# One product per block in a convolution over frequencies, and column halves for the last rows of three output projections

## What is computed

```python
def rms_norm_2(x, g):
    xf = x.astype(jnp.float32)
    y = xf * lax.rsqrt(jnp.mean(xf * xf, axis=-1, keepdims=True) + RMS_EPS)
    return (y * g.astype(jnp.float32)).astype(x.dtype)
...
    u = a_val * jax.nn.sigmoid(a_gate)
    u = depthwise_conv_centred(u, conv_w, conv_b)
...
    y = jnp.concatenate([y_a, y_b], axis=-1) @ w_out
    return x + rms_norm_2(y, g_post)
```

## Time and profile before

| | |
|---|---|
| median of 3 runs | 897.77 us |
| the profiled execution's own time | 897.9 us |
| its span, first to last instruction | 896.1 us |
| PE busy | 865.1 us, 97% of the span |
| DVE busy | 533.7 us, 60% |
| ACT busy | 487.8 us, 54% |
| mean granted clock of PE | 0.992 of full speed |

### The profile page before, as it was taken

How to read it: one execution, slowest core, us unless ns; L and a number is a source line. 1 busy time by engine, 2 the same in 40 slices (tenths; PEclk the granted TensorE clock), 3 DMA queues, 4 the chain that set the end, 5 groups by cost and what they waited for, 6 DMA issues and landing times.

```text
span 896.1 us, 15443 instructions
## 1 busy us (share of the span) xinstructions
PE 865.1 (97%) x6204; PEld 787.0 (88%) x6204; DVE 533.7 (60%) x947; ACT 487.8 (54%) x819; POOL 18.5 (2%) x23
## 2 busy tenths in 40 slices
PE   8999999999999999999899999999999799999996
PEld 7999898879689999988699998899988699998785
DVE  5344347757666666666765344268775654548664
ACT  6653456763474445454653244746675565445453
POOL 0000000006100000000000000000000000000000
PEclk9999999999999999999999999999999999999999
DMA  9655732335445555555445244333436454535211
GB/s 363 254 183 191 282 139 95 112 125 198 150 138 184 188 189 188 185 187 193 141 147 183 94 142 142 129 132 122 157 120 244 140 176 154 189 101 181 95 48 70
DMA packets 21698, 144.53 MB, mean 161 GB/s; under 512 B 2529, under 2 KB 3169, under 8 KB 4992
## 3 DMA queue, kind: packets, MB, share of 16 engines
q1 hardware_dynamic: 20736, 140.55, 45.3%
q10 hardware_dynamic: 896, 3.03, 1.0%
HBM read 142.53 MB, written 1.05 MB: 160 GB/s over the span
## 4 chain that ended last, share of the span: by engine, by line
PE 87%; DVE 5%; ACT 4%; DMA 2%; issue 1%; DVEq 0%; ACTq 0%
PE PS L424 85%; DVE wl L1672 2%; ACT wh L1153 2%; DMA ring<-w 1%; ACT PB L1187 1%; DMA xa<-x 0%; PE PS L1069 0%; ACT hh L1167 0%; PE PS L695 0%; DVE PB L2155 0%; PE PS L697 0%; PE PS L696 0%; DVE PB L1715 0%; DVE hl L1692 0%; DVE cn L1976 0%
## 5 line engine op out<-in xcount | busy, mean ns | idle before, releaser
L1672 DVE TENSOR_TENSOR wl<-ring,wh 128x1024 fp32r<-128x1024 f32 x248 | 305.6, 1235 | 293.5 <-ACT wh L1153 293.2
L1153 ACT ACTIVATE wh<-ring 128x1024 fp32r<-128x1024 f32 x248 | 261.5, 1056 | 269.1 <-PE PS L424 250.6
L424 PE MATMUL PS<-hh,wh 128*128 128x256 f32 x1244 | 359.1, 289 | 2.5 <-DVE hl L1729 2.2
L424 PE MATMUL PS<-hl,wh 128*128 128x256 f32 x1244 | 352.5, 283 | 0.0
L424 PE MATMUL PS<-hh,wl 128*128 128x256 f32 x1244 | 352.4, 283 | 0.0
L424 PEld LDWEIGHTS PS<-hh,wh 128*128 128x128 f32 x1244 | 238.9, 192 | 8.1 <-issue 5.4
L424 PEld LDWEIGHTS PS<-hl,wh 128*128 128x128 f32 x1244 | 239.0, 192 | 1.4 <-issue 1.2
L424 PEld LDWEIGHTS PS<-hh,wl 128*128 128x128 f32 x1244 | 238.9, 192 | 0.0
L424 PE MATMUL PS<-wh,hh 128*128 128x256 f32 (+2 forms) x496 | 171.0, 345 | 5.2 <-DVE hl L1692 4.1
L424 PE MATMUL PS<-wl,hh 128*128 128x256 f32 (+2 forms) x496 | 166.9, 337 | 0.0
L424 PE MATMUL PS<-wh,hl 128*128 128x256 f32 (+2 forms) x496 | 166.9, 337 | 0.0
(11 more groups left out here) (266 smaller groups left out, 710.2 us busy)
## 6 DMA issues: line engine op xcount, KB each, us to landing
ring<-w SPq DMA_DIRECT2D x127, 1024.0 KB, 4.8
cn<-consts SPq DMA_DIRECT2D x2, 1051.0 KB, 9.5
V<-gains ACTq DMA_DIRECT2D x3, 512.0 KB, 6.2
cn<-consts SPq DMA_DIRECT2D x1, 1050.5 KB, 9.1
xa<-x SPq DMA_DIRECT2D x2, 512.0 KB, 4.5
ring<-w SPq DMA_DIRECT2D x2, 512.0 KB, 5.8
out<-xb SPq DMA_DIRECT2D x4, 256.0 KB, 2.1
cn<-late ACTq DMA_DIRECT2D x1, 704.0 KB, 8.1
```

Of the source, the lines that this page charges most:

```text
L424: return nc.tensor.matmul(o, lhsT, rhs, start=start, stop=stop, skip_group_check=True)
L1153: A(wh[:, q % SPLITS, :], ring[:, i % RING, e:e + HALF], ACT.Copy).then_inc(sem("hi_ready"), 1)
L1672: TTn(wl[:, q % SPLITS, :], ring[:, PLACE[unit_of(q)] % RING, e:e + HALF], wh[:, q % SPLITS, :].bitcast(F32), ALU.subtract).then_inc(sem(" ...
```

## The change

In the convolution DVE makes the sum that PE made: it multiplies the spectrum by `WF[0]` into `z`, multiplies each half of the partitions by `WF[1]` into the other half of `turned`, and adds `turned` to `z`. The sign moves into the table `conv_tap`. `conv_inverse` has one matmul where it had two. The second set is done at i == 1 of the loop, ahead of the gate biases, instead of at i == 2 behind them.

In the three output projections the last rows of t = 1 are done by column halves: h = 0 for the last three halves of weights (`first_rows` again), then h = 1 with the releases. ACT squares each column half by itself (`part_square`); DVE adds epsilon to the first half's sum (`part_bias`), and the root takes that as its bias (`part_root`). At two joins the split of the next matrix's first half goes behind the norm's work on ACT (`down`) and on DVE (`down` and `even_out`).

```diff
             def deep(first, a, b, bank):
...
+            def deep_last_rows(first, rest, bank):
+
+                for k in rest:
+                    m = deep_part(first, k, 1, 0, bank)
+                m.then_inc(sem("first_rows"), 1)
+                for k in rest:
+                    half_out(deep_part(first, k, 1, 1, bank))
...
-                        for k in range(2):
-                            m = mm(PS[:, AV[i % 2], e * S + o:e * S + o + n], PRODUCT[i // 2][:, b, k, q:q + P],
-                                   c("conv_inv", k * BLOCK, k * BLOCK + n), k == 0, k == 1)
+                        m = mm(PS[:, AV[i % 2], e * S + o:e * S + o + n], PRODUCT[i // 2][:, b, 0, q:q + P],
+                               c("conv_inv", 0, n), True, True)
...
+            def part_square(m, h, src):
+
+                o = (spare if m == 3 else xh[:, 1, :])[:, h * 512:(h + 1) * 512]
+                A(o, src, ACT.Square, scale=D ** -0.5,
+                  accum_out=ssq[:, TT * m + 1:TT * m + 2] if h else stat[:, 42 + m % 2:43 + m % 2])\
+                    .then_inc(sem("row_ssq[1]"), 1)
+
+            def part_root(m):
+
+                act.wait_ge(sem("row_ssq[1]"), PARTS_DONE[m, 1])
+                act.wait_ge(sem("row_bias"), m)
+                A(rms[:, TT * m + 1:TT * m + 2], ssq[:, TT * m + 1:TT * m + 2], ACT.Sqrt,
+                  bias=stat[:, 44 + m % 2:45 + m % 2]).then_inc(sem("row_rms[1]"), 1)
...
-            act.wait_ge(sem("first_rows"), 3)
+            act.wait_ge(sem("first_rows"), 4)
             row_square(4, 0, PS[:, EVEN_AT:EVEN_AT + 2, :])
             row_root(4, 0)
+            act.wait_ge(sem("first_rows"), 5)
+            part_square(4, 0, PS[:, EVEN_AT + 2, :])
             halves(half_of("lora") + 1)
             act.wait_ge(sem("half_used"), half_of("even_out") + 16)
-            row_square(4, 1, PS[:, EVEN_AT + 2:EVEN_AT + 4, :])
-            row_root(4, 1)
-            for t in range(TT):
-                act.wait_ge(sem("x4_ready"), t + 1)
-                row_square(5, t, cols2(xa[:, t, :]))
-                row_root(5, t)
+            part_square(4, 1, PS[:, EVEN_AT + 3, :])
+            part_root(4)
+            act.wait_ge(sem("x4_ready"), 1)
+            row_square(5, 0, cols2(xa[:, 0, :]))
+            row_root(5, 0)
+            for h in range(2):
+                act.wait_ge(sem("x4_ready"), h + 2)
+                part_square(5, h, xa[:, 1, h * 512:(h + 1) * 512])
+            part_root(5)
...
-                    for i in range(2):
-                        ins = TTn(PRODUCT[h][:, b, i, :], PS[:, 3 + b, :], WF[i][h], ALU.mult)
-                    ins.then_inc(sem("conv_weighed"), 1)
+                    z, turned = PRODUCT[h][:, b, 0, :], PRODUCT[h][:, b, 1, :]
+                    own(TTn(z, PS[:, 3 + b, :], WF[0][h], ALU.mult))
+                    for lo in (0, SPAN):
+                        q, o = slice(lo, lo + SPAN), slice(SPAN - lo, P - lo)
+                        own(TTn(turned[o], PS[q, 3 + b, :], WF[1][h][q], ALU.mult))
+                    settled()
+                    TTn(z, z, turned, ALU.add).then_inc(sem("conv_weighed"), 1)
...
                 halves(half_of("qk") + i + 1 + SPLITS)
+                if i == 1:
+                    weigh_spectrum(1)
                 if i == 2:
...
-                if i == 2:
-                    weigh_spectrum(1)
...
-            for t in range(TT):
-                gained(6, DEEP, t)
-                post_norm(6, t, xa, xb, "out_ready", 2)
+            gained(6, DEEP, 0)
+            post_norm(6, 0, xa, xb, "out_ready", 2)
+            part_gained(6, DEEP, 0)
+            part_bias(6)
+            part_gained(6, DEEP, 1)
+            post_norm(6, 1, xa, xb, "out_ready", 2)
...
-    put_conv("conv_tap", np.concatenate([cos, cos, sin, sin], 1))
+    put_conv("conv_tap", np.concatenate([cos, cos, sin, -sin], 1))
     cos, sin = (q.T / P for q in turn(np.arange(BLOCK)))
-    put_conv("conv_inv", np.concatenate([np.concatenate([cos, -sin]), np.concatenate([-sin, -cos])], 1))
+    put_conv("conv_inv", np.concatenate([cos, -sin]))
```

More of the change, by code:

```diff
@@ L299, in program @@
         xh = PBF[:, 0:TT * D].rearrange("p (t d) -> p t d", t=TT)
+        spare = PBF[:, TT * D:(TT + 1) * D]
         gB = V[:, 0, :]
@@ L504, in normed, with deep_part @@
                 activations("h_split", KD * n)
+            def deep_part(first, k, t, h, bank):
+                wh_, wl_ = half_in(half_of(first) + k)
+                q, c_ = slice(t * P, (t + 1) * P), slice(h * 512, (h + 1) * 512)
+                return three(PS[:, bank + 2 * t + h, :], hh[:, k % 8, q], hl[:, k % 8, q], wh_[:, c_], wl_[:, c_],
+                             k == 0)
             def deep_rows(first, k, t, bank):
-                wh_, wl_ = half_in(half_of(first) + k)
                 if t == 0:
                     pe.wait_ge(sem("deep_split"), DEEP0[first] + k + 1)
[L511 to L516, removed]
+                deep_part(first, k, t, 0, bank)
+                return deep_part(first, k, t, 1, bank)
             def deep_half(first, k, bank):
@@ L527, in deep @@
                     deep_half(first, k, bank)
-                for k in range(rest, b):
-                    m = deep_rows(first, k, 0, bank)
                 if rest < b:
+                    for k in range(rest, b):
+                        m = deep_rows(first, k, 0, bank)
                     m.then_inc(sem("first_rows"), 1)
-                for k in range(rest, b):
-                    half_out(deep_rows(first, k, 1, bank))
+                    deep_last_rows(first, range(rest, b), bank)
             def taps_turned(i):
@@ L1102, in _ @@
             m.then_inc(sem("first_rows"), 1)
-            for k in (9, 10, 11):
-                half_out(deep_rows("odd_out", k, 1, DEEP))
+            deep_last_rows("odd_out", (9, 10, 11), DEEP)
         def ahead(split_half):
@@ L1986, in _, with joined @@
             dve.wait_ge(sem("gains_in"), 16)
[L1988 to L1990 removed]
+            def joined(i, t, a, b):
+                src = PS[:, DEEP + 2 * t + a // 512:DEEP + 2 * t + b // 512, :]
+                TTn(cols2(xa[:, t, a:b], (b - a) // 512), src, cols2(xb[:, t, a:b], (b - a) // 512), ALU.add)\
                     .then_inc(sem("x2_ready"), 1)
[L1992 to L1999, removed]
[L2001 to L2009 removed]
+                dve.wait_ge(sem("x2_ready"), i + 1)
+                TTn(xb[:, t, a:b], xa[:, t, a:b], gB[:, a:b], ALU.mult).then_inc(sem("gained"), 1)
+            dve.wait_ge(sem("first_rows"), 2)
+            joined(0, 0, 0, D)
+            dve.wait_ge(sem("first_rows"), 3)
+            joined(1, 1, 0, 512)
+            dve.wait_ge(sem("row_ssq[0]"), 3)
+            TS(stat[:, 40:41], ssq[:, 4:5], EPS, EPS * EPS, ALU.mult, ALU.add).then_inc(sem("row_bias"), 1)
+            dve.wait_ge(sem("half_used"), half_of("down") + NF)
+            joined(2, 1, 512, D)
+            scaled(3, 0, xb)
+            part_bias(2)
+            dve.wait_ge(sem("row_ssq[1]"), PARTS_DONE[3, 0])
+            own(STT(stat[:, 46:47], stat[:, 42:43], EPS, stat[:, 43:44], ALU.mult, ALU.add))
+            settled()
+            own(TS(stat[:, 46:47], stat[:, 46:47], EPS * EPS, None, ALU.add))
+            settled()
+            dve.wait_ge(sem("row_ssq[1]"), PARTS_DONE[2, 1])
+            STT(stat[:, 45:46], ssq[:, 5:6], EPS, stat[:, 46:47], ALU.mult, ALU.add).then_inc(sem("row_bias"), 1)
+            scaled(3, 1, xb)
+            halves(half_of("conv_in") + 1)
             turned_evac(2, "g3", half_of("conv_in"))
@@ L2169, in _ @@
             post_norm(4, 0, xb, xa, "x4_ready", 1)
+            part_gained(4, EVEN_AT, 0)
+            part_bias(4)
+            part_gained(4, EVEN_AT, 1)
+            post_norm(4, 1, xb, xa, "x4_ready", 2)
+            scaled(5, 0, xa)
+            part_bias(5)
+            scaled(5, 1, xa)
             halves(half_of("lora") + 1)
-            gained(4, EVEN_AT, 1)
-            post_norm(4, 1, xb, xa, "x4_ready", 1)
-            for t in range(TT):
-                scaled(5, t, xa)
             turned_evac(3, "g4", half_of("lora"))
```

46 lines of the change are left out of this document (33 added, 13 removed).

## The result

The changed kernel took **890.92 us** (median of 5 runs, 889.06 to 892.16) against 897.77 us (5 runs, 896.72 to 898.69): a ratio of 0.9923, with a 95% interval of 0.9912 to 0.9935. The forecast was 890.8 us. The profiled execution took 889.9 us, its span 888.1 us; before they were 897.9 and 896.1.

What follows compares the result with a forecast made beforehand. PE was taken to bound the kernel, busy 865.1 of 896.1 us. The terms -5.2 + 0.2 - 0.45 - 0.9 - 0.95 + 0.3 = -7.0 us gave 890.8 us from 897.77, range 888.6 to 893.4 us.

Steps and rivals of the forecast that it cites:

- The convolution on PE: In `conv_inverse`, half of about 96 matmul records go, each with its own weight load: -5.2 us.
- The set of twelve on DVE: In the convolution, twelve products and sums per weighing take 8.4 us, bounds 7.7 and 8.8.
- The stall at half 15: In `conv_in`, PE waits for a split behind the first DVE set, with 8.2 us free: +0.2 us, bounds 0 and 0.6.
- No stall at the second set: In the convolution, the earlier second set has 8.95 us free, so no stall at 8.4 or 8.8 us.
- The join behind `down`: Scaled rows begin at 448.1 instead of 448.55, with half a square at 0.7 us: -0.45 us.
- Behind `even_out`: In that join, half squares and half gain products start norm 5's rows at 715.05 instead of 715.94: -0.9 us.
- at the end: Behind `odd_out`, the last sums start at 891.25 instead of 892.21: -0.95 us.
- The clock: In both inner joins the half-speed stretch stays put and earlier matmuls fall into it: +0.3 us.
- The rival in which the shorter joins close the gap: Shorter PE pauses in the joins let the transposes run at full speed: 888.0 to 889.6 us; chance 10%.
- The dear weighing: In the DVE sets, crossing operations cost 1.0 us each, with stalls of 2.0 + 1.2: 893.8 us; chance 10%.
- the slower case: In the DVE sets, crossing products cost over twice a normal one, from 1.33 us each; 900 us at 1.5; chance 3%.
- the rival that the joins give nothing: In the joins, each half of a square costs nearly a whole one: 892.8 us; chance 7%.

Runs made afterwards that it cites:

- alternate: The changed kernel, but the six products on 64 partitions write to the partitions they read (output not the convolution); a single run took 888.94 us.
- old_place: The changed kernel with the second weighing behind the gate biases (i == 2), as before; a single run took 896.53 us.
- after_again: The changed kernel, unchanged, run once more beside its variants on the same chip; 891.49 us, ratio 0.9927.
- grouped: The changed kernel with the twelve DVE operations of a set ordered by kind instead of by block; 888.26 us, ratio 0.9899.
- joins_only: The kernel before with only the column halves in the three output projections, old convolution; 894.82 us against 897.51, ratio 0.9973.
- busy_halves: The kernel before with only the column halves, plus unread matmuls in PE's pauses; 892.75 us.
- busy_after: The changed kernel with only unread matmuls in PE's pauses added; 888.02 us.
- busy_joins: The kernel with DVE operations ordered by kind (grouped), plus unread matmuls in PE's pauses; 887.50 us, ratio 0.9883.

## Why the prediction was right, step by step

**The convolution on PE** held: -5.2 forecast, 10.47 to 5.12 us, so -5.35. A dropped matmul took its weight load with it: in the three windows PEld has 51 records instead of 99.

**The set of twelve on DVE** was forecast at 8.4 us between bounds of 7.7 and 8.8, and took 8.55. The rule of the Trainium skill (VectorE: DVE Perf Modes, section "Two Vector instructions with no wait between them") is that an instruction is held until the earlier ones have finished when an input of it starts in another group of 32 partitions than the first input that was last read from the same memory, or its output in another group than the last output there. It told the distances better than my choice. By it I had estimated 8.8 us, with 0.73 us for each from the earlier trace rows; the distance is 0.72. Where the operations start at 0 or 64 the experiments bear it out, the unheld product of alternate included. Eleven distances of 0.72 and 0.61 from the last sum to the split make the 8.55. The 8.4 us had no reckoning of their own, but were a choice between the bounds.

**The stall at half 15** is the term that was mis-sized: +0.2 us forecast, 0.69 measured on PE. The set's time accounts for 0.15 of the difference. Another 0.1 is the slower start of PE behind the wait, which the sum didn't have. The rest is the free time, where "at about 498.8 PE enters half 15" failed as a reading. That is the moment at which ACT was released by the half before, and ACT sees it later than PE goes on: in the trace of before the first matmul of half 15 starts at 498.54, and in this one ACT's row of 497.45 stands against 497.17 for PE, 0.28 us later in both. That is what the profile gives as the length of such a matmul (0.28 us), whose end ACT waits for. The free time was 7.95 us, not 8.2; 8.55 less 7.95 is the 0.60 us by which PE started late.

**No stall at the second set**: right, but by 0.15 us and not by the 0.55 of the forecast, since 528.1 was read from ACT's row in the same way. At the rule's 8.8 us there would have been one. That the late ACT costs nothing was right. But "at the old place it would have stood one split later" named the wrong waiter: old_place showed PE waiting 2.8 us for the sums themselves. The earlier place is worth much more than I had seen, as far as a single run shows.

**The join behind `down`**: -0.45 forecast, -0.84 measured. I took 0.7 us for half a square; it is 0.61 us from start to start (444.67 to 445.28), with the accumulator's record inside it. Four of them make 0.36 of the 0.39 missing. **Behind `even_out`** -0.9 against -0.95, **at the end** -0.95 against -1.01: right, and for the reason given, half a square and half a gain product less on the path.

**The clock** was forecast at +0.3 us. With it kept full the change is worth 7.45 us; left to itself it was 6.85 us here and 898.14 - 891.49 = 6.65 with after_again. So the medians put 0.6 to 0.8 us of the gain down to the clock, about the bound of 0.65. This isn't clear of noise: the interval of the first comparison (0.9912 to 0.9935) is a gain of 5.8 to 7.9 us, and 7.45 lies in it. The way I told is wrong in any case. "The stretch at half speed stays where it is" isn't what happens: behind `down` it is there in after_again and missing in the changed kernel's first trace, in the odd half of the layer it is there before and missing after, and behind `even_out` it differs in length. The rival in which the shorter joins close the gap came true in one join of one run (behind `down`), and not in the median. I had named a full clock in the joins as a sign that the forecast is wrong; in that run the gain there was made up by the loss behind `even_out`.

**The sum.** -5.35 + 0.69 - 0.84 - 0.95 - 1.01 = -7.46 us, against -7.45 with a full clock. The 0.6 us from there to the measured -6.85 are the clock's by difference, and no separate check. The mechanism of the forecast held in every term but the clock's. That -7.0 lies within 0.2 us of the result is luck in part: the convolution gave 0.15 us more than forecast, the join behind `down` 0.4 and the other two places 0.1, while the stall took 0.5 us and the clock 0.3 us more. The dear weighing (1.0 us for a crossing product) is refuted by grouped, where such a product takes 0.6 us; with it falls the slower case. Of the rival that the joins give nothing, joins_only and busy_halves leave nothing.

## What to carry to other kernels

Put VectorE operations that start at the same partition together: by kind instead of by block, the same twelve took 7.58 instead of 8.55 us, and a stall of 0.7 us of TensorE went. When the margin is in tenths of a us, read when an engine enters a stage from its own rows, not from the row of the engine that it releases. And where runs of one kernel spread by 3 us with the granted clock, fill TensorE's pauses with matmuls that nobody reads: the median fell by 2.3 us for the kernel before, 2.9 for the changed one and 0.8 for grouped, and the gains of the change's parts, measured so, add up to within 0.2 us.

## What had not been expected

The kernel's spread, 889.06 us at a mean clock of 0.994 to 892.16 at 0.989, goes with TensorE's clock and nearly vanishes when the clock is kept full, though in the traces of the kernel before and of the changed one the clock falls only in and behind the joins, and in that of before in the odd half of the layer. With the pauses filled, the kernel before gains 2.3 us (897.75 to 895.47) and the changed one 2.9 (890.92 to 888.02), and the runs of busy_after and of busy_joins agree within 0.3 us. The order by kind on DVE is worth 0.69 us, the whole stall: from `conv_in` to `even_out` lie 203.99 us in the trace of busy_joins and 204.68 in that of busy_after (the medians, 887.50 and 888.02, are of two chips). The other 2.5 of the 3.2 us between grouped and after_again would then be the clock's, by difference: grouped kept it at 0.992 to 0.996 in five of six runs, the changed kernel at 0.989 to 0.995. That isn't shown, and why grouped should keep it up more often, with the same pauses, stays open.
